# Turning the gated units with the tokens of the expert after next, and taking the rotary rows turned from their projections

## What is computed

```python
q_mla = einsum(_rms_norm(c_q, g), w_mla_q_up[l])      # 4 heads x (64 + 32) columns
q_full = concatenate([q_mla[..., :64], _rope(q_mla[..., 64:], positions)])
k_rope = _rope(k_rot, positions)                      # 32 columns, shared by the heads

def _rope(x, positions):                              # half = 16
    x1, x2 = x[..., :half], x[..., half:]
    return concatenate([x1 * cos - x2 * sin, x1 * sin + x2 * cos])
```

```python
xs = h[idx]                                           # gathered rows
y = (silu(xs @ w_gate) * (xs @ w_up)) @ w_down        # scattered back, times the affinity
```

## Time and profile before

| | us |
|---|---|
| median of 3 runs | 2929.48 |
| lowest, highest run | 2926.32, 2931.20 |
| the profiled execution's own time | 2931.33 |
| its span, first to last instruction | 2929.2 |
| TensorE matmuls busy | 2571.7 (88%) |
| VectorE, ScalarE, GpSimd busy | 1000.6, 731.1, 234.7 |

### The profile page before, as it was taken

How to read it: one execution, slowest core, us unless ns; L and a number is a source line. 1 busy time by engine, 2 the same in 40 slices (tenths; PEclk the granted TensorE clock), 3 DMA queues, 4 the chain that set the end, 5 groups by cost and what they waited for, 6 DMA issues and landing times. The chain is left out here.

```text
span 2929.2 us, 42755 instructions
## 1 busy us (share of the span) xinstructions
PE 2571.7 (88%) x17010; PEld 1363.5 (47%) x17010; DVE 1000.6 (34%) x2212; ACT 731.1 (25%) x1889; POOL 234.7 (8%) x276
## 2 busy tenths in 40 slices
PE   7999999999989889896999999948899969878784
PEld 3564644664646567554444444425565533222221
DVE  3022440213345664557111222136652551111112
ACT  2234311333321344422111211122342320100010
POOL 1000100000101001011000000001100110100000
PEclk9999999999999999997999999978899969999998
DMA  7343615343613001116799999971102069999997
GB/s 223 85 131 88 171 42 144 102 130 97 178 37 87 1 14 52 43 58 245 269 400 401 401 396 398 377 197 36 28 1 79 37 258 385 405 398 405 407 405 281
DMA packets 270524, 577.71 MB, mean 197 GB/s; under 512 B 12512, under 2 KB 203328, under 8 KB 221248
## 3 DMA queue, kind: packets, MB, share of 16 engines
q1 hardware_dynamic: 257088, 530.78, 49.6%
q0 software_dynamic: 13168, 45.08, 5.5%
q10 hardware_dynamic: 144, 0.14, 0.0%
HBM read 552.84 MB, written 23.10 MB: 197 GB/s over the span
## 5 line engine op out<-in xcount | busy, mean ns | idle before, releaser
L450 PE MATMUL ps<-turned,ring 128*128 128x512 f32 (+1 forms) x1408 | 553.7, 554 | 10.2 <-ACT turned L1452 8.8
L1084 PE MATMUL ps<-ring,turned 128*32 128x512 f32 (+1 forms) x2208 | 379.5, 608 | 47.9 <-DMA ring<-in_w_gate 45.8
L450 PEld LDWEIGHTS ps<-turned,ring 128*128 128x128 f32 x1408 | 271.1, 194 | 281.5 <-issue 261.2
L1245 DVE SCALAR_TENSOR_TENSOR turned<-turned,gates,work 64x1024 f32<-64x1024 f32 (+1 forms) x48 | 61.3, 1276 | 501.6 <-ACT turned L1184 280.8
L695 PE MATMUL ps<-ring,mixT 128*128 128x512 f32 x512 | 223.9, 597 | 0.8 <-DVE mixT L1610 0.8
L496 PE MATMUL ps<-kz,qz 96*128 96x256 f32 (+3 forms) x384 | 164.3, 515 | 23.1 <-DVE qz L2027 8.7
L1084 PEld LDWEIGHTS ps<-ring,turned 128*32 128x32 f32 (+1 forms) x2208 | 92.3, 120 | 190.2 <-DMA ring<-in_w_gate 79.7
L1161 ACT ACTIVATE work<-ps 128x512 f32<-128x512 f32 x32 | 19.1, 597 | 574.5 <-PE ps L1084 294.2
L1638 ACT ACTIVATE probs_v<-ps,col 128x256 f32<-128x256 f32 (+5 forms) x216 | 136.5, 632 | 74.0 <-DVE col L1588 37.8
L1651 ACT ACTIVATE probsT<-ps 128x512 f32<-128x512 f32 (+3 forms) x280 | 120.3, 456 | 134.4 <-PE ps L536 103.0
L695 PEld LDWEIGHTS ps<-ring,mixT 128*128 128x128 f32 x512 | 96.8, 191 | 118.6 <-issue 117.3
(11 more groups left out here) (270 smaller groups left out, 3154.1 us busy)
## 6 DMA issues: line engine op xcount, KB each, us to landing
ring<-in_w_gate SPq DMA_DIRECT2D x120, 1024.0 KB, 13.6
ring<-in_w_up SPq DMA_DIRECT2D x64, 1024.0 KB, 14.0
mixT<-in_w_up SPq DMA_DIRECT2D x64, 1024.0 KB, 14.1
ring<-in_w_mod SPq DMA_DIRECT2D x96, 512.0 KB, 4.0
ring<-in_w_in SPq DMA_DIRECT2D x82, 512.0 KB, 7.3
mixcT<-in_w_down SPq DMA_DIRECT2D x32, 1024.0 KB, 12.7
probs_v<-in_w_down SPq DMA_DIRECT2D x32, 1024.0 KB, 14.3
qz<-in_w_down SPq DMA_DIRECT2D x32, 1024.0 KB, 16.6
```

The costliest lines, as they stand in the source:

```text
L450: mm = nc.tensor.matmul(ps[:, b, 0:n], w[:, k, :], rhs[:, k, 0:n], start=(k == 0), stop=(k == KD - 1))
L1084: mm = nc.tensor.matmul(ps[o:o + step, dst, :], lhs[:, k, g:g + step], w[:, half * 512:(half + 1) * 512], start=(k == 0), stop=(k == KD - ...
L1245: ins = nc.vector.scalar_tensor_tensor(ye[R, :], ye[R, :], g, grow[R, r, :], ALU.mult, ALU.mult)
```

## The change

It has two parts.

**Rotary rows.** The weights are loaded a second time with the two halves of the rotary columns swapped, to the columns 96 to 127 of `wmisc` and of each head of `wqup`, so that the projections give both the rows and the swapped rows, in the partitions 64 to 95 and 96 to 127. The sign is in the table of sines, which moves to the rows 96 to 127. The jobs "krr" and "mqr" go. VectorE's first instruction of each turn reads the swapped rows in SBUF instead of PSUM, and the keys' turn comes ahead of the scaling by the roots. GpSimd issues four more DMAs for `wmisc` and five more for `wqup` in each layer, no longer clears `kr`, and copies the turned key rows after its squares.

**Experts.** The tokens of expert e + 2 are turned in round e, right after the gated units of e; the gate product of e + 1 runs its eight steps in one piece. The evacuations move with it: VectorE's modulation behind the copy of the turned units, ScalarE's behind the gate's activation. GpSimd gathers the tokens of e + 3 in round e, ahead of its scatter. The tokens of expert 1 are turned before the first round. One more round is written out at the end (two for all engines but SyncE, three for GpSimd).

```diff
@@ shape_constants
-        c[o:o + half, C_SIN:C_SIN + SEQ] = np.sin(ang)
+    c[KROWS:KROWS + half, C_SIN:C_SIN + SEQ] = -np.sin(ang)
+    c[KROWS + half:P, C_SIN:C_SIN + SEQ] = np.sin(ang)
@@ pe_first_block
-            job = ("krr", l)
-            b = open_job(pe, job)
-            pe.wait_ge(*emptied(("misc", l)))
-            nc.tensor.matmul(ps[0:KROWS, b, :], const[0:KROWS, C_ROTM:C_ROTM + KROWS], kr[0:KROWS, :], start=True,
-                             stop=True).then_inc(*done("job_done", job))
...
-                    mm = nc.tensor.matmul(ps[0:MLA_QK, b, :], wqup[:, c, hh * MLA_QK:(hh + 1) * MLA_QK], cqT[:, c, :],
+                    mm = nc.tensor.matmul(ps[:, b, :], wqup[:, c, hh, :], cqT[:, c, :],
...
-            for hh in range(HEADS):
-                job = ("mqr", l, hh)
-                b = open_job(pe, job)
-                pe.wait_ge(*emptied(("mqu", l, hh)))
-                nc.tensor.matmul(ps[0:KROWS, b, :], const[0:KROWS, C_ROTM:C_ROTM + KROWS], qz[0:KROWS, hh, :],
-                                 start=True, stop=True).then_inc(*done("job_done", job))
@@ pe_experts
             gate(0, range(KD))
+            pe.wait_ge(*nth("gathered", l, 1, 16))
+            turn_xs(1)
 
             def body(e):
-                if more_after(e):
-
-                    count = settled(pe, nth("gathered", l, e + 1, 16)[1])
-                    pe.wait_ge(*emptied(("topT", l)))
-                    pe.wait_ge(sem("gathered"), count)
-                    turn_xs(e + 1)
...
-                    gate(e + 1, range(KD // 2))
+                    gate(e + 1, range(KD))
...
-                if more_after(e):
-                    gate(e + 1, range(KD // 2, KD))
+                if more_after(e, 2):
+
+                    count = settled(pe, nth("gathered", l, e + 2, 16)[1])
+                    pe.wait_ge(*emptied(("topT", l)))
+                    pe.wait_ge(sem("gathered"), count)
+                    turn_xs(e + 2)
...
-            rounds(pe, body)
+            rounds(pe, body, last=EXPERTS - 2)
@@ experts_act, body
                 if more_after(e):
-                    act.wait_ge(*nth("xsT_kept", l, e))
-                    modulate(e + 1)
                     gated(e + 1)
+                if more_after(e, 2):
+                    act.wait_ge(*nth("xsT_kept", l, e + 1))
+                    modulate(e + 2)
@@ experts_dve, body
-                if more_after(e):
-                    dve.wait_ge(*nth("xsT_kept", l, e))
-                    modulate(e + 1)
-
...
                 ins.then_inc(sem("hidT"), 1)
+                if more_after(e, 2):
+                    dve.wait_ge(*nth("xsT_kept", l, e + 1))
+                    modulate(e + 2)
@@ experts_pool, body
-                if more_after(e, 2):
-                    pool.wait_ge(*nth("xs_turned1", l, e + 1))
-                    gather(e + 2)
+                if more_after(e, 3):
+                    pool.wait_ge(*nth("xs_turned1", l, e + 2))
+                    gather(e + 3)
@@ dve_first_block, ahead of the scaling by the roots
+            R, B = slice(HD, KROWS), slice(KROWS, P)
+
+            def rotate(name, job, x):
+
+                dve.wait_ge(*at("evac_act", job))
+                nc.vector.tensor_tensor(rope_t[R, :], cst(C_SIN, SEQ, B), x[B], ALU.mult).then_inc(*done("dve_step", ("rs", l, name)))
+                nc.vector.tensor_tensor(x[R], x[R], cst(C_COS, SEQ, R), ALU.mult).then_inc(*done("dve_step", ("rc", l, name)))
+                dve.wait_ge(*at("dve_step", ("rs", l, name)))
+                dve.wait_ge(*at("dve_step", ("rc", l, name)))
+                nc.vector.tensor_tensor(x[R], x[R], rope_t[R, :], ALU.add).then_inc(
+                    *(done("kr_roped", l) if name == "k" else done("mla_q", (l, name))))
...
+            rotate("k", ("misc", l), kr)
@@ dve_first_block, behind it
+            for hh in range(HEADS):
+                rotate(hh, ("mqu", l, hh), qz[:, hh, :])
@@ gpsimd
-            nc.gpsimd.memset(kr[:, :], 0.0)
...
+                    for to, o in ((KROWS, ROPE // 2), (KROWS + ROPE // 2, 0)):
+                        pool.dma_start(wmisc[:, kk, to:to + ROPE // 2],
+                                       w_cols(a["w_in"], l, O_KR + o, ROPE // 2)[:, kk, :]).then_inc(sem("misc_landed"), 16)
+                for k in range(2):
+                    heads = a["w_mla_q_up"][l, k * P:(k + 1) * P, :].rearrange("p (h c) -> p h c", h=HEADS)
+                    for to, o, n in ((0, 0, MLA_QK), (KROWS, HD + ROPE // 2, ROPE // 2), (KROWS + ROPE // 2, HD, ROPE // 2)):
+                        pool.dma_start(wqup[:, k, :, to:to + n], heads[:, :, o:o + n]).then_inc(sem("mla_landed"), 16)
...
                 pool.wait_ge(*at("kr_roped", l))
+                pool.wait_ge(*at("squares", (l, 1)))
```

More of the change, by code:

```diff
@@ L220, in build_program @@
         wmisc = hcf[:, 0:1024].rearrange("p (k n) -> p k n", k=KD)
-        wqup = hcf[:, 1024:1024 + 2 * HEADS * MLA_QK].rearrange("p (k n) -> p k n", k=2)
+        wqup = hcf[:, 1024:1024 + 2 * HEADS * P].rearrange("p (k h n) -> p k h n", k=2, h=HEADS)
         hp = work[:, 0:2 * (SEQ + 2 * HALO)].rearrange("p (c n) -> p c n", c=2)
@@ L752, in pe_first_block @@
                         pe_head(pe, ("plain", -1), t)
-            pe.wait_ge(sem("misc_landed"), 64 * (l + 1))
+            pe.wait_ge(sem("misc_landed"), 128 * (l + 1))
             job = ("misc", l)
@@ L1169, in experts_act @@
             gated(0)
+            act.wait_ge(*nth("xsT_kept", l, 0))
+            modulate(1)
             def body(e):
                 if more_after(e):
-                    act.wait_ge(*nth("xsT_kept", l, e))
-                    modulate(e + 1)
                     gated(e + 1)
+                if more_after(e, 2):
+                    act.wait_ge(*nth("xsT_kept", l, e + 1))
+                    modulate(e + 2)
                 act.wait_ge(*rows_used(l, "down", e, KD - 1))
@@ L1186, in body @@
                 ins.then_inc(sem("ye_copied"), 1)
-            rounds(act, body)
+            rounds(act, body, last=EXPERTS - 2)
         def experts_dve(dve, l):
@@ L1213, in experts_dve @@
             keep(0)
+            dve.wait_ge(*nth("xsT_kept", l, 0))
+            modulate(1)
             dve.wait_ge(*emptied(("grow", l, 1, 1 if l == 0 else 0, 1)))
             def body(e):
-                if more_after(e):
-                    dve.wait_ge(*nth("xsT_kept", l, e))
-                    modulate(e + 1)
                 dve.wait_ge(*rows_used(l, "up", e, KD - 1))
@@ L1246, in body @@
                 ins.then_inc(sem("ye_scaled"), 1)
-            rounds(dve, body)
+            rounds(dve, body, last=EXPERTS - 2)
         def experts_pool(pool, l, load_rows):
@@ L1271, in experts_pool @@
             load_rows(("experts", l), a["ln2_g_2"][l], a["ln2_b_2"][l])
+            pool.wait_ge(*nth("xs_turned1", l, 1))
+            gather(2)
             def body(e):
-                if more_after(e, 2):
-                    pool.wait_ge(*nth("xs_turned1", l, e + 1))
-                    gather(e + 2)
+                if more_after(e, 3):
+                    pool.wait_ge(*nth("xs_turned1", l, e + 2))
+                    gather(e + 3)
                 if not is_number(e) or e > 0 or l > 0:
@@ L1291, in body @@
                     in_=ye[0:rows, :], in_offset=None, compute_op=ALU.add).then_inc(sem("scattered"), 16)
-            rounds(pool, body, last=EXPERTS - 2)
+            rounds(pool, body, last=EXPERTS - 3)
         RESIDUALS = {"residual_stored_c": (NT, NT + 1), "residual_stored_a": (0, 1), "residual_stored_b": (2, 3)}
@@ L1723, in act_first_block @@
                                  bias=vec[0:HEADS, V_BF + l:V_BF + l + 1]).then_inc(*done("f_logit", l))
-            nc.scalar.activation(kr[HD:KROWS, :], ps[HD:KROWS, b, :], ACT.Copy).then_inc(*done("evac_act", job))
+            nc.scalar.activation(kr[HD:P, :], ps[HD:P, b, :], ACT.Copy).then_inc(*done("evac_act", job))
             act.wait_ge(*at("f_logit", l))
@@ L1771, in act_first_block @@
                 act.wait_ge(*at("job_done", job))
-                nc.scalar.activation(qz[0:MLA_QK, hh, :], ps[0:MLA_QK, bank_of(job), :], ACT.Copy,
+                nc.scalar.activation(qz[:, hh, :], ps[:, bank_of(job), :], ACT.Copy,
                                      scale=MLA_QK ** -0.5).then_inc(*done("evac_act", job))
@@ L1881, in dve_first_block @@
             dve_stick(dve, l)
+            R, B = slice(HD, KROWS), slice(KROWS, P)
[7 more added lines that the diff above has]
+                    *(done("kr_roped", l) if name == "k" else done("mla_q", (l, name))))
+                dve.wait_ge(*(at("kr_roped", l) if name == "k" else at("mla_q", (l, name))))
+            rotate("k", ("misc", l), kr)
             for i, (name, job) in enumerate((("kv", ("kvsum", l)), ("q", ("qsum", l)))):
@@ L1894, in dve_first_block @@
                 ins.then_inc(*done("rms_ready", (l, name)))
-            R = slice(HD, KROWS)
-            cos, sin = cst(C_COS, SEQ, R), cst(C_SIN, SEQ, R)
```

(11 more changed lines are left out.)

3 lines of the change are left out of this document (1 added, 2 removed).

## The result

The changed kernel takes **2915.07 us** (median of 7 runs, 2907.75 to 2921.95) against 2930.63 us of the kernel before (7 runs beside it, 2926.32 to 2934.36): ratio 0.9948, 95% interval 0.9935 to 0.9960. That is 15.6 us less, where 8.4 us were forecast, and just outside the range of 2916.5 to 2926.0. The profiled execution took 2914.22 us (span 2912.4), 17.1 less than the profiled one of before.

A forecast was written before the change was run, and what follows sets the result against it. It took TensorE to bound layer 0's experts and the latent attention, and weights to bound layer 1's experts. Terms -8.8 + 1.3 - 1.8 + 0.9 = -8.4 us took 2929.5 to 2921.1 us, range 2916.5 to 2926.0.

The forecast's parts named there:

- the extra DMAs: GpSimd's nine more DMAs a layer, 7.6 us, were to lie in a gap of 28.66 us and cost nothing.
- the price of a merged turn: Layer 0's experts: turning units and tokens together saves one switch, 0.13 us in each of fourteen experts, 1.8 us.
- Rotary jobs leave TensorE's queue: Latent attention: without the keys' and queries' rotary turns TensorE saves 4.4 us a layer, 8.8 us in two.
- GpSimd's copies hold up VectorE: Latent attention: copies of turned key rows slow VectorE's L1888, delaying the key projections; 1.3 us lost (0 to 2.4).
- I take the value of the row, 0.65: Delay of the key projections per layer, priced from a similar VectorE instruction elsewhere that took 1.85 us beside GpSimd.
- Queries' turns are covered: Latent attention: VectorE's turns of the queries end at 297.4, with 4 us of cover under TensorE's modulation jobs.
- The fifteenth expert: Layer 0: with no tokens left to turn, the copy of the turned units is bared once, 0.9 us lost.
- Layer 1's experts, nothing: Layer 1's expert stage is bound by its weights, whose bytes and order stay, so no change in time.
- Rival A: Layer 0's experts: the copy of the turned units shows, 0.3 us in each of fourteen; 2925.3 us, chance 0.13.
- B: Latent attention gives back part: VectorE's query turns or blocked L1888 set the time; 2923.8 us, chance 0.10.
- C: Layer 0's experts: the clock falls after each merged turn, slowing one step by 1.1 us; 2936.7 us, chance 0.04.
- D: Switch saves nothing and the rotary jobs stood where TensorE would wait anyway; within 0.2% of before, chance 0.05.

## Why the prediction was wrong in size

The sign and the two places were right, and three of its terms; the sum was too small by 7. Two steps failed: that the extra DMAs cost and change nothing (point 3), and the price of a merged turn (point 4). A third was wrong the other way round from the whole, a loss that did not come (point 2).

1. *Rotary jobs leave TensorE's queue, 8.8 us.* Right: 8.7 by the rows (4.36 a layer with the blocking of point 2 at zero, 4.4 forecast).
2. *GpSimd's copies hold up VectorE, 1.3 us given back.* Wrong: 0. The step that failed is "I take the value of the row, 0.65". The row was of other sizes (GpSimd's 2.83 us on 1024 columns) and another order of starts, and in this place GpSimd's copies paid, not VectorE. The scores' start moved by 4.36, not 3.7, and L1888 stayed at 0.75. The price was also mis-added: a scaling of 1.85 us from 279.67 ends at 281.52, 0.57 after 280.95, not 0.65.
3. *Queries' turns are covered, the extra DMAs cost nothing.* The turns: right, VectorE begins them at 288.02 us and ends at 296.9, with the scores at 301.22. The DMAs: right where they are issued. The step that failed is "Nothing" for the rest of their queue: with the rotary part GpSimd's stores hundreds of microseconds later come 0.67 us later, and the stall near 790 us is gone. That is the largest part of the error, 5.4 us in the first pair of profiles and 4.3 on the mean of the eight with the stall, and it was luck that it is in our favour. The prediction looked at the clears that are queued directly behind the DMAs, and no further. That the pause comes from the DMAs, and not from another edit of the rotary part, isn't shown.
4. *A merged turn saves 0.13 us.* The step that failed took the cost of a turn from the steps between the turns alone (15.62 against 15.48 us). After the change the 24 steps take 32.96 - 1.86 = 31.10 us instead of 2 x 15.62 = 31.24, which is the forecast 0.14; but the turns themselves take 1.86 instead of 1.13 + 0.92 = 2.05, 0.19 less: the units' turn 1586.03 - 1585.21 = 0.82, and the tokens' 1587.07 - 1586.03 = 1.04. An interval from the first turned block to the next product holds a share of the switch too, and adding two of them counts it twice. For fourteen experts 4.5 us, not 1.8.
5. *The fifteenth expert, 0.9 us.* Right: 0.88.
6. *Layer 1's experts, nothing.* Right for the period (32.12 and 32.05 us). In this pair of profiles the stage took back 1.7 us of the lead with which it began (18.5 ahead at its start, 16.8 at the end). From its first turned token to the last scaling it takes 495.6 to 498.6 us in five profiles with the experts' part and 494.7 to 497.6 in five without, so whether any of the 1.7 is the change's isn't shown.

8.7 + 5.4 + 4.5 - 0.9 - 1.7 = 16.0 us, against 15.6 to 16.7 by the medians. The sum is close in part by luck: it leaves out 1.0 us gained at the start of the kernel, 3.4 lost ahead of the experts and 3.1 gained between the two expert stages, which differ from execution to execution, and with 4.3 in place of 5.4 it would be 14.9. Rival A did not come (no idle before a down product but the fifteenth's), B not (0.70 us before the scores, for a modulation row), C not (clock 1.00), D not.

## What to carry to other kernels

Count a switch between kinds of work by the period of the loop, not by adding up pieces of it: each piece has a way in or out. When an edit adds DMAs to a queue, look at the places where that queue is next used beside time-critical work, however far away: here two stores that come 0.67 us later were worth 4.3 us on the mean, as much as all the removed products of a layer. And before a gain is put down to what was removed, undo it in halves and look where in the program the time was won.

## What the runs showed of the hardware

Where two stores of 8 KB were issued by GpSimd right behind 1 MB of loads and just ahead of SyncE's next loads of weights, ScalarE and VectorE were held for some microseconds, and TensorE behind them, in eight of eight profiles; with the stores 0.66 us or more later they were not, in ten of ten. The stall had an echo: TensorE's granted clock fell behind it in seven of the eight, and in this place in none of the ten.

Half-clocked stretches also go with part of the spread of 8 to 14 us between runs of one kernel: of the change's seven runs the fastest, 2907.75 us, has a mean granted clock of 0.958, and the slowest, 2921.95, of 0.953. At 725 to 745 us the first and the third profile of the kernel before differ mainly in this (windows of the two profiles):

```profile
725.00:745.00 20.00, 18.57 (x129) 11.69 (x128) 15.95 (x54) 13.35 (x44) 2.05 (x2) 1.00 0.94 248
```
```profile
725.00:745.00 20.00, 19.61 (x92) 11.29 (x92) 12.07 (x42) 10.28 (x37) 0.00 (x0) 0.66 0.82 217
```

The upper row is the first profile. The same kernel, the clock at 1.00 in the one and at a mean of 0.66 in the other, and by VectorE's matching rows 6.1 us lost there. So a single profile pair can differ by this much at such a place, and only a place that differs in every pair, like the one near 790 us, belongs to the change.
